# Loading an expert's weights in four transfers instead of six

## What is computed

```
h = rmsnorm(x);  u, q, k, v = h @ w_in
x = x + concat([pool_mixer(u), dilated_attention(q, k, v)]) @ w_out
h2 = rmsnorm(x)
gates, experts = softmax(top_4(h2 @ router_w + router_b))
for each expert e, over the tokens that chose it:
    gate, up = split(h2[tokens] @ w_gate_up[e] + b_gate_up[e])     # 1024 x 2048
    act = (clip(up, -7, 7) + 1) * min(gate, 7) * sigmoid(1.702 * min(gate, 7))
    y = act @ w_down[e] + b_down[e]                                # 1024 x 1024
x = x + sum over the four experts of gate * y
out = rmsnorm(x)
```

## Time and profile before

| | |
|---|---|
| median of three runs | 1345.72 us |
| profiled execution: its time | 1345.49 us |
| its span in the profile | 1343.5 us |
| PE busy | 1196.4 us, 89% |
| DVE busy | 522.3 us, 39% |
| POOL busy | 228.9 us, 17% |
| ACT busy | 180.9 us, 13% |
| queue 1 (SP's transfers) | 430.53 MB in 33726 packets, 76.8% of the sixteen engines' span |
| queue 0 (POOL's transfers) | 22.09 MB in 9568 packets, 4.4% |
| granted TensorE clock, mean | 0.946 |

### The profile page before, as it was taken

The page is one execution under the profiler, slowest core; times in us unless marked ns, Lnnn a source line. Parts: engine busy times, 40 slices in busy tenths (PEclk is TensorE's granted clock), DMA queues, the critical chain, the costliest instruction groups (busy, mean ns, idle before and its releaser), DMA issues.

```text
span 1343.5 us, 24712 instructions
## 1 busy us (share of the span) xinstructions
PE 1196.4 (89%) x8892; PEld 449.7 (33%) x8893; DVE 522.3 (39%) x1449; ACT 180.9 (13%) x338; POOL 228.9 (17%) x233
## 2 busy tenths in 40 slices
PE   7998998986999999999999988889996898878775
PEld 6743554452332322333333322223331232212221
DVE  2002322244544444444445443334443343534336
ACT  2113332210010111111110100001110010100012
POOL 0054443001111111111111111121112021111110
PEclk9998999987999999999999988889999898988898
DMA  9422201056899999999999999999999999999847
GB/s 378 172 95 78 94 17 63 32 225 257 325 426 426 425 423 425 424 425 426 425 425 420 426 425 426 424 425 419 421 411 424 425 405 425 417 426 421 353 160 313
DMA packets 44012, 455.16 MB, mean 339 GB/s; under 512 B 8161, under 2 KB 8457, under 8 KB 17110
## 3 DMA queue, kind: packets, MB, share of 16 engines
q1 hardware_dynamic: 33726, 430.53, 76.8%
q0 software_dynamic: 9568, 22.09, 4.4%
q10 hardware_dynamic: 696, 2.25, 0.5%
HBM read 444.56 MB, written 16.81 MB: 343 GB/s over the span
## 4 chain that ended last, share of the span: by engine, by line
PE 63%; DMA 29%; DVE 3%; POOL 2%; issue 1%; ACT 1%; SPq 0%; DVEq 0%; POOLq 0%; ACTq 0%
PE bank L703 32%; DMA arena<-in_w_gate_up 24%; PE bank L731 10%; PE bank L481 5%; PE bank L555 4%; PE bank L499 3%; PE bank L722 3%; DMA arena<-in_w_down 2%; DMA arena<-y_rows 1%; PE bank L542 1%; PE bank L514 1%; PE bank L528 1%; PE bank L457 1%; PE bank L682 1%; PE bank L636 1%
## 5 line engine op out<-in xcount | busy, mean ns | idle before, releaser
L703 PE MATMUL bank<-arena,hT 128*32 128x512 f32 x5120 | 585.6, 611 | 44.6 <-DMA arena<-in_w_gate_up 40.6
L703 PEld LDWEIGHTS bank<-arena,hT 128*32 128x32 f32 x5120 | 160.7, 112 | 437.9 <-issue 382.1
L731 PE MATMUL bank<-arena,hT 128*64 128x512 f32 x1024 | 247.9, 641 | 48.1 <-DVE hT L1297 48.1
L731 PEld LDWEIGHTS bank<-arena,hT 128*64 128x64 f32 x1024 | 75.5, 146 | 213.5 <-issue 144.8
L1036 POOL DMA_INDIRECT y_rows<-hT,arena x32 | 32.7, 1022 | 594.5 <-DVE hT L1330 577.1
L914 ACT ACT_TABLE_LOAD x48 | 61.6, 1283 | 532.2 <-issue 531.9
L1285 DVE TENSOR_TENSOR arena<-bank,gain 128x512 f32<-128x512 f32 x80 | 55.4, 692 | 182.3 <-PE bank L703 182.3
L1012 POOL DMA_INDIRECT hT<-h_rows,arena x82 | 83.5, 1019 | 248.7 <-issue 142.8
L481 PE MATMUL bank<-hT,arena 128*128 128x512 f32 x224 | 103.7, 611 | 0.0
L914 ACT ACTIVATE arena<-arena 128x256 f32<-128x256 f32 x80 | 33.3, 416 | 355.5 <-DVE arena L1287 355.5
L1330 DVE TENSOR_TENSOR hT<-bank,gain 128x512 f32<-128x512 f32 x32 | 22.1, 692 | 130.6 <-PE bank L731 130.6
(11 more groups left out here) (150 smaller groups left out, 757.5 us busy)
## 6 DMA issues: line engine op xcount, KB each, us to landing
arena<-in_w_gate_up SPq DMA_DIRECT2D x128, 2048.0 KB, 25.0
arena<-in_w_down SPq DMA_DIRECT2D x64, 2048.0 KB, 20.5
arena<-in_w_in SPq DMA_DIRECT2D x10, 1024.0 KB, 16.6
arena<-y_rows SPq DMA_DIRECT2D x8, 1024.0 KB, 12.5
arena<-in_w_out SPq DMA_DIRECT2D x4, 1024.0 KB, 15.4
arena<-bias_by_dist POOLq DMA_DIRECT2D x6, 512.0 KB, 3.9
xs<-in_x SPq DMA_DIRECT2D x4, 512.0 KB, 8.2
h_rows<-arena POOLq DMA_DIRECT2D x4, 512.0 KB, 2.9
```

What stands on the lines that cost most here:

```text
L703: mm = pe.matmul(bank[c][j * CH:(j + 1) * CH, :].rearrange("p (g n) -> p g n", g=2), xT[:, c, k * CH:(k + 1) * CH], w[:, :, j * Q:(j + 1) ...
L731: mm = pe.matmul(bank[3][g * 2 * CH:(g + 1) * 2 * CH, :], aT_pair[:, k].rearrange("p c s -> p (c s)"), w[:, g * 2 * Q:(g + 1) * 2 * Q], st ...
```

## The change

A table `GROUPED` of (first unit, number of units) takes the place of the pairs: units 0 to 3 are one transfer of 128 rows of 32 KB, 4 MB; units 4, 5 and 6, 7 stay as they are; units 8 to 11 are one transfer of 4 MB. Each group has one semaphore. SP waits for all slots of a group to be read before it issues, and PE waits for a whole group at its first unit. Ahead of the loop, units 8 to 11 of job 0 are issued together after `op_done`. The order of the groups is the order of the pairs, and the bytes are the same.

```
-EARLY = 4
+GROUPED = ((0, 4), (4, 2), (6, 2), (8, 4))
...
-            def wait_read(job, u, low=None):
+            def wait_read(job, u, n, low=None):
 
-                if u + 2 == KT:
+                if u + n == KT:
                     sp.wait_ge(gu_done, low + AHEAD)
-                elif u + 2 == JOB_UNITS:
+                elif u + n == JOB_UNITS:
                     sp.wait_ge(dn_done, low + AHEAD)
                 else:
-                    sp.wait_ge(units_used, job * FREED + (u + 2 - (u >= KT)))
+                    sp.wait_ge(units_used, job * FREED + u + n)
...
-            def load_two(e, u, half):
+            def load_group(e, u, n, half):
                 if u < KT:
-                    src = w_gate_up[bass.ds(e, 1)].rearrange("e (p m k) n -> (e m) p (k n)", p=P, k=2)[u // 2]
+                    src = w_gate_up[bass.ds(e, 1)].rearrange("e (p m k) n -> (e m) p (k n)", p=P, k=n)[u // n]
                 else:
-                    src = w_down[bass.ds(e, 1)].rearrange("e (p m k) n -> (e m) p (k n)", p=P, k=4)[(u - KT) // 2]
+                    src = w_down[bass.ds(e, 1)].rearrange("e (p k) n -> e p (k n)", p=P)[0]
                 a = ring_slot(half, u)
-                sp.dma_start(ring[:, a:a + 2, :].rearrange("p u n -> p (u n)"), src).then_inc(two_full[u // 2], 16)
+                sp.dma_start(ring[:, a:a + n, :].rearrange("p u n -> p (u n)"), src).then_inc(group_full[u], 16)
...
-            sp.wait_ge(out_used, 2)
-            load_two(0, 8, 0)
             sp.wait_ge(op_done, TT)
-            load_two(0, 10, 0)
+            load_group(0, 8, 4, 0)
...
-            ahead, rest, late = range(0, EARLY, 2), range(EARLY, HALF, 2), range(HALF, JOB_UNITS, 2)
+            ahead, rest, late = GROUPED[0:1], GROUPED[1:2], GROUPED[2:4]
...
                 for k in range(KT // 2):
-                    if k % 2 == 0:
-                        pe.wait_ge(two_full[k // 2], full)
+                    if k == 0:
+                        pe.wait_ge(group_full[0], full)
...
                 for k in range(KT):
-                    if k % 4 == 0:
-                        pe.wait_ge(two_full[(KT + k // 2) // 2], full)
+                    if k == 0:
+                        pe.wait_ge(group_full[KT], full)
                     down_pair(k)
```

More of the change, by code:

```diff
@@ L262, in program @@
         mix_full = [sem(f"mix_full{s}") for s in range(MIX_RING)]
-        two_full = [sem(f"two_full{u}") for u in range(0, JOB_UNITS, 2)]
+        group_full = {u: sem(f"group_full{u}") for u, n in GROUPED}
         units_used = sem("units_used")
@@ L364, in ring_slot @@
                 return u + JOB_UNITS if half and u < HALF else u
-            def wait_read(job, u, low=None):
-                if u + 2 == KT:
+            def wait_read(job, u, n, low=None):
+                if u + n == KT:
                     sp.wait_ge(gu_done, low + AHEAD)
-                elif u + 2 == JOB_UNITS:
+                elif u + n == JOB_UNITS:
                     sp.wait_ge(dn_done, low + AHEAD)
                 else:
-                    sp.wait_ge(units_used, job * FREED + (u + 2 - (u >= KT)))
-            def load_two(e, u, half):
+                    sp.wait_ge(units_used, job * FREED + u + n)
+            def load_group(e, u, n, half):
                 if u < KT:
-                    src = w_gate_up[bass.ds(e, 1)].rearrange("e (p m k) n -> (e m) p (k n)", p=P, k=2)[u // 2]
+                    src = w_gate_up[bass.ds(e, 1)].rearrange("e (p m k) n -> (e m) p (k n)", p=P, k=n)[u // n]
                 else:
-                    src = w_down[bass.ds(e, 1)].rearrange("e (p m k) n -> (e m) p (k n)", p=P, k=4)[(u - KT) // 2]
+                    src = w_down[bass.ds(e, 1)].rearrange("e (p k) n -> e p (k n)", p=P)[0]
                 a = ring_slot(half, u)
-                sp.dma_start(ring[:, a:a + 2, :].rearrange("p u n -> p (u n)"), src).then_inc(two_full[u // 2], 16)
-            for n in range(0, KT, 2):
-                sp.wait_ge(proj_done, groups_before(IN_UNITS - KT + n + 2))
-                load_two(0, n, 0)
-            sp.wait_ge(out_used, 2)
-            load_two(0, 8, 0)
+                sp.dma_start(ring[:, a:a + n, :].rearrange("p u n -> p (u n)"), src).then_inc(group_full[u], 16)
+            for u, n in GROUPED[0:3]:
+                sp.wait_ge(proj_done, groups_before(IN_UNITS - KT + u + n))
+                load_group(0, u, n, 0)
             sp.wait_ge(op_done, TT)
-            load_two(0, 10, 0)
-            for n in range(0, HALF, 2):
-                if n == HALF - 2:
+            load_group(0, 8, 4, 0)
+            for u, n in GROUPED[0:2]:
+                if u:
                     sp.wait_ge(ssq_done, 2 * TT)
@@ L395, in _ @@
                         sp.wait_ge(h2_out[b], 16 * TT // 2)
-                sp.wait_ge(two_full[n // 2], 16)
-                load_two(1, n, 1)
+                sp.wait_ge(group_full[u], 16)
+                load_group(1, u, n, 1)
             sp.wait_ge(jobs_done, 2)
             def load_part(e, job, half, units, free_of, low=None):
-                for u in units:
-                    wait_read(free_of, u, low)
+                for u, n in units:
+                    wait_read(free_of, u, n, low)
                     sp.sem_inc(waited_sp, 1)
-                    sp.wait_ge(two_full[u // 2], job * 16)
+                    sp.wait_ge(group_full[u], job * 16)
                     sp.sem_inc(waited_sp, 1)
-                    load_two(e, u, half)
+                    load_group(e, u, n, half)
             def counted(job):
@@ L714, in gate_rest @@
                         if c > 0 and k % 2 == 0:
-                            pe.wait_ge(two_full[k // 2], full)
+                            pe.wait_ge(group_full[k], full)
                         gate_step(c, k)
```

## The result

The changed kernel takes 1348.26 us (median of 10 runs, 1346.78 to 1351.32), the kernel before 1345.43 us in the runs beside it (10 runs, 1343.40 to 1346.21). The ratio is 1.0029 with a 95% interval of 1.0018 to 1.0040, which is +3.9 us (2.4 to 5.4). It was forecast at 1350.2, or +4.5 us. The profiled execution took 1347.20 us, its span is 1345.3 us.

The account below looks back on a forecast made before the run. DMA bytes were taken to set the pace in the jobs, with PE waiting for units 6, 7. The terms 3.0 + 4 - 2.5 + 0 + 0 = +4.5 us gave 1350.2 us, range 1345.0 to 1355.0.

Parts of the forecast that it names:

- 1, units 8, 9 later: Start of the unbroken stream: units 8, 9 of job 1 wait for the end of job 0's down product, +3.0 us.
- 2, traffic ahead of the routing: Before PE starts job 0: 2.1 MB more queued ahead of h2's gathers, +4 us, between 0 and +9.4.
- The row of the loaded gather: Last gather of job 0: in a full queue it takes 7.4 us instead of 3.3, +4.1 us.
- the question that the prediction left open: Last h2 store: whether rows of 32 KB delay it, +5.3 us if that part doubles, or leave it as it is.
- 3, fewer packets: Unbroken stream: 59 merged pairs save up to 0.09 us each; -2.5 us taken, between 0 and -5.3.
- the first rival: Not slower: packets save the full 0.09 us per pair, added queue ahead of gathers near 0; 1343.4 us at best, chance 0.25.
- 4, the stream isn't interrupted: Every job: units 8, 9 asked for 3.3 to 3.5 us later, but 6.2 us of queued work covers it; 0.
- 5, PE's down waits: Down products: PE waits for all four down units, but later waits for units 6, 7 shrink; 0 at the end.
- The rival by which they bind: PE's new down waits of 1.5 to 3 us in four to six jobs aren't taken back: 1360 us, chance 0.06.
- The signs: Profile after: PE's first gate weights near 320 us, later h2 store, 8192 rows fewer in queue 1, DMA share still 1.0.
- One of my own marks of failure: Prediction wrong if job 3's first units to the last ones isn't within 5 us of its old length.
- The fixed price of a transfer: Rival: each transfer costs 2.5 us beside its bytes, so 59 merged pairs save 147 us: 1206 us, chance 0.02.

## Why the prediction was right

The direction and the size were right, 1348.3 for 1350.2, inside 1345.0 to 1355.0. The steps:

- **1, units 8, 9 later, +3.0.** Right. 3.1 us in the profile of after, and 3.0 in both of its profiles once the first 96 products are taken out of b; 2.9 in that of the experiment that has this alone (3.45 without them), 3.6 (1.8 to 5.5) by its time.
- **2, traffic ahead of the routing, +4 (0 to 9.4).** Right, somewhat low: +5.7 and +5.5 us in two profiles. The row of the loaded gather, 4.1, was the right one for the moved bytes (4.5 alone, by the profile), and the length of a row, which I took at nothing for the store, made the rest. Where both act they share the work: the store's path to the first gather grows by 3.4 us (309.90 - 292.37 = 17.53, before 14.14), the last gather by 2.7 and not 4.1. The traces answer the question that the prediction left open: longer rows do delay the store (13.58 us for 10.36 with no byte moved). The Trainium skill ("DMA: Bandwidth & Descriptors", section "SWDGE vs HWDGE vs iDMA") has an engine change queues at the end of a packet, of at most 4096 B preferably. Were the packets that short here, the length of a row would be nothing to the store, and these waits disagree, 8.68, 10.36 and 15.76 us for rows of 8, 16 and 32 KB; with a row as one packet, as the profile counts them, they don't contradict the switch at a packet's end.
- **3, fewer packets, -2.5 (0 to -5.3).** This term was mis-sized. It was worked out as 59 x 0.09 = 5.3 us and then halved, for fear of cut rows and of rounded windows. Rows of 32 KB go uncut, and the stream became 5.9 and 4.9 us shorter, the whole price; the experiment with 8 KB rows gives 9.3 ns for each of 1488 packets. The 10 ns from two windows with an eightfold difference in packets were better than I held them to be. It was not the forecast but the first rival that had this half right; of that rival only the other half (term 2 near 0) failed.
- **4, the stream isn't interrupted, 0.** Right: share 1.00, no slice under 410 GB/s from 370 to 1244 us, and s unchanged when only the wait moves (932.12 for 932.77).
- **5, PE's down waits, 0 at the end.** Right in the sum and wrong in what they look like. I had forecast 1 to 3 us each, followed by shorter waits for units 6, 7. They are up to 5.9 us, since PE's place of waiting has for the most part moved here and the 3.0 us for DVE are inside them. In the chain of after the down transfers stand where units 6, 7 did; before, then after:

```profile
1234.65 26.09 DMA arena<-in_w_gate_up
...
1220.63 21.06 DMA arena<-in_w_down
...
1241.82 9.25 PE bank L729 x32
```

  The rival by which they bind would have been 1360. The down-only run, with 77.7 us of them, has a stream shorter than before.
- **The sum.** 3.0 + 5.6 - 5.4 = +3.2 us by the profiles, 3.9 (2.4 to 5.4) by the runs. Term 2 came out 1.6 us higher and term 3 2.9 us lower than taken, so two misses of opposite sign cancel in part; the forecast was off by less than either. That part of its closeness is luck.
- **The signs.** The rows in queue 1 fell by 8192 as said (and 1024 semaphore writes with them), PE starts at 320.65 for "near 320", and the store lands late (15.9 us after its issue, 10.5 before). One of my own marks of failure was met: the stretch from the first units of job 3 to the last ones was to keep its length within 5 us. By their issues it went from 1280.66 - 354.10 = 926.56 to 1282.13 - 361.88 = 920.25 us, 6.3 shorter. The mark was drawn too narrow: my own term 3 reached to -5.3, and a shorter stretch is that term and no sign against the mechanism.
- The fixed price of a transfer is refuted: 59 pairs merged in the stream gave 5.4 us in place of 147. The Trainium skill ("DMA: Bandwidth & Descriptors", section "Anatomy of one DMA") gives 2.0 us for a transfer that GpSimd issues; used for SP's transfers, as the prediction did, it would have been an estimated 118, and the runs disagree for transfers that queue.

## What to carry to other kernels

When a kernel runs at the pace of its DMA queue, ask three things of a merged transfer: when the unbroken stream now begins, how many packets it saves (here 10 ns each on every engine, even at 16 KB), and which small transfer of another queue stands behind its longer rows. The gain comes from the packets and the loss from the one place where the queue had been empty, so a hold at that place can turn the sign. Waits that grow inside the stream are to be read by the period of the loop, not by their sum.

## What the runs showed of the hardware that I had not expected

With the other queue full, its rows lengthen a small transfer. The gathers land after a median of 7.4 us with 16 KB rows throughout, 8.0 with units 0 to 3 in rows of 32 KB (the held gates-only run), 8.7 with the down units in them (the down-only run) and 9.1 with both (the kernel after). The last three:

```profile
DMA to landing us min/median/max: 2.5/8.0/13.8
...
DMA to landing us min/median/max: 3.3/8.7/12.1
...
DMA to landing us min/median/max: 3.0/9.1/12.1
```

For rows of 8 KB the trace has landings of job 0's three gathers only (4.9 to 6.2 us, before 3.3 to 4.9), where the queue runs empty, so it doesn't say how long a gather takes in a full queue of them.

The rows of 32 KB alone, with no byte moved, lengthen the wait for the h2 store from 10.36 to 13.58 us. And the price of a packet doesn't fade with its size: it is 9 to 10 ns between 8 and 16 KB and again between 16 and 32 KB.

After 10 us in which PE was busy for 0.4 to 1.4 us, at a granted clock of 0.50, the same 96 products took 11.81 to 13.47 us, with a clock of 0.90 to 0.78 in the 13.5 us from their start. Two executions of one kernel stand at the two ends, so a single profile can hide or feign 1.7 us there.
